# Second sweep of the down projection: pairs in another order, the other accumulators added in two halves, gains on GpSimd, and row tile 0 scaled by two engines

## The reference

```
u = rms_norm(x, ln2) @ w_ffn_in              # 2048 x 11264
a, b = split(u)
g = gelu(causal_depthwise_conv(a)) * b       # 256 x 5632
x = x + g @ w_ffn_out                        # 5632 x 2048: the down projection
y = rms_norm(x, ln_f)                        # x * rsqrt(mean(x^2) + eps) * ln_f
```

## Time and profile before

| what | value |
|---|---|
| median of three executions | 1091.71 us |
| the profiled execution's own time | 1091.31 us |
| its span, first to last instruction | 1089.5 us |
| busy: TensorE, VectorE, ScalarE, GpSimd | 1077.2, 831.9, 602.1, 81.7 us |
| share of TensorE in the span | 99% |
| DMA rate over the span | 253 GB/s |
| mean granted TensorE clock | 0.997 of full speed |

### The profile page before, as it was taken

One profiled execution on the slowest core, in us unless ns is written; L12 is line 12 of the kernel. 1 busy time (PEld: TensorE's weight loads), 2 busy tenths in 40 slices (PEclk: granted clock), 3 DMA queues, 4 the chain that ended last, 5 costly groups with the idle time before them and its releaser, 6 DMA issues.

```text
span 1089.5 us, 16759 instructions
## 1 busy us (share of the span) xinstructions
PE 1077.2 (99%) x5777; PEld 920.9 (85%) x5777; DVE 831.9 (76%) x1117; ACT 602.1 (55%) x810; POOL 81.7 (7%) x86
## 2 busy tenths in 40 slices
PE   9999999999999999999999999999999999999996
PEld 7888888888888888888888888888888888888884
DVE  5755777666768577968879678686798988888897
ACT  7445555555555454544545445455454777777774
POOL 2000111111100000101101011010010100000000
PEclk9999999999999999999999999999999999999998
DMA  9766555555599688797897987978877599969992
GB/s 341 267 190 191 162 168 159 155 171 166 165 317 357 177 267 305 229 337 252 281 320 233 318 266 254 355 209 321 285 236 276 179 315 323 301 223 317 319 325 102
DMA packets 163352, 276.06 MB, mean 253 GB/s; under 512 B 9091, under 2 KB 77537, under 8 KB 159984
## 3 DMA queue, kind: packets, MB, share of 16 engines
q1 hardware_dynamic: 162448, 273.39, 75.5%
q0 software_dynamic: 544, 1.69, 0.4%
q10 hardware_dynamic: 320, 0.47, 0.1%
HBM read 248.18 MB, written 27.26 MB: 253 GB/s over the span
## 4 chain that ended last, share of the span: by engine, by line
PE 93%; DVE 3%; DMA 2%; ACT 1%; issue 0%; SPq 0%; ACTq 0%; DVEq 0%
PE acc L703 16%; PE acc L611 11%; PE acc L613 11%; PE acc L612 11%; PE acc L711 8%; PE bank_s L703 8%; PE bank_tr L703 8%; PE bank_tr L711 4%; PE bank_s L711 4%; DMA raw<-in_w_ffn_out 1%; PE bank_s L613 1%; PE bank_s L611 1%; PE bank_s L612 1%; PE bank_tr L613 1%; PE bank_tr L612 1%; PE bank_tr L611 1%
## 5 line engine op out<-in xcount | busy, mean ns | idle before, releaser
L974 ACT ACTIVATE w_hi<-raw 128x1024 fp32r<-128x1024 f32 x292 | 309.5, 1061 | 404.6 <-PE acc L613 135.7
L1271 DVE TENSOR_TENSOR w_lo<-raw,w_hi 128x1024 fp32r<-128x1024 f32 x292 | 356.1, 1224 | 186.4 <-ACT w_hi L974 185.5
L703 PE MATMUL acc<-h_both,w_hi 128*128 128x512 f32 x768 | 238.4, 392 | 0.0
L703 PEld LDWEIGHTS acc<-h_both,w_hi 128*128 128x128 f32 x768 | 137.9, 189 | 23.2 <-DVE rstd_row L1649 0.2
L711 PE MATMUL acc<-h_both,w_lo 128*128 128x256 f32 x768 | 154.2, 282 | 0.0
L711 PEld LDWEIGHTS acc<-h_both,w_lo 128*128 128x128 f32 x768 | 125.9, 191 | 7.5
L703 PE MATMUL bank_s<-h_both,w_hi 128*128 128x512 f32 x384 | 118.6, 390 | 0.0
L703 PE MATMUL bank_tr<-h_both,w_hi 128*128 128x512 f32 x384 | 118.6, 390 | 0.0
L611 PE MATMUL acc<-w_hi,h_both 128*128 128x512 f32 (+1 forms) x288 | 111.9, 389 | 0.9 <-DVE h_both L1285 0.9
L613 PE MATMUL acc<-w_hi,h_both 128*128 128x512 f32 (+1 forms) x288 | 109.0, 378 | 0.0
L612 PE MATMUL acc<-w_lo,h_both 128*128 128x512 f32 (+1 forms) x288 | 108.8, 378 | 0.0
(11 more groups left out here) (278 smaller groups left out, 1722.9 us busy)
## 6 DMA issues: line engine op xcount, KB each, us to landing
raw<-in_w_ffn_in SPq DMA_DIRECT2D x176, 512.0 KB, 4.4
raw<-in_w_in SPq DMA_DIRECT2D x130, 256.0 KB, 3.0
raw<-in_w_ffn_out SPq DMA_DIRECT2D x64, 512.0 KB, 6.2
stage<-in_w_ffn_out SPq DMA_DIRECT2D x24, 1024.0 KB, 8.2
kept_sums<-stage SPq DMA_DIRECT2D x24, 1024.0 KB, 6.7
raw<-kept_sums SPq DMA_DIRECT2D x24, 768.0 KB, 6.0
raw<-in_w_out SPq DMA_DIRECT2D x32, 512.0 KB, 4.7
raw<-in_w_in SPq DMA_DIRECT2D x19, 512.0 KB, 9.2
```

The lines of the kernel that those rows point to most:

```text
L703: ins = mm(banks[ft // 2][:, ft % 2, :], w_hi[:, slot, q * COLS + ft * P:q * COLS + (ft + 1) * P], h_both[:, 2 * k + q, :, :].rearrange("p ...
L974: run(w_hi[:, n % SPLIT, :], raw[:, n % RAW, :], ACT.Copy).then_inc(hi_ready, 1)
L1271: tt(w_lo[:, n % SPLIT, :], raw[:, n % RAW, :], w_hi[:, n % SPLIT, :].bitcast(F32), ALU.subtract).then_inc(lo_ready, 1)
```

## The change

Five things, all in the second sweep and at its end:

1. The second sweep's pairs come in another order (`ORDER`, `k_pair`). Before, its sevens stood at r = 25, 26, 28, 29, 31, 32, 34, 35, 37, 38, 40, 41. Now they stand at r = 24, 25, 27, 28, 30, 31, 32, 34, 35, 37, 38, 39, and r = 40 to 43 are eights. So twice three sevens follow one another.
2. The other accumulators of the second sweep are added at r = 41 (three additions) and r = 42 (three more), after the low parts of these steps, where they wait for r = 39.
3. The load of `ln_f` is issued behind the loads of r = 40, and ahead of those of r = 41.
4. The four products of the first sweep's blocks with `ln_f` go from VectorE (r = 40) to GpSimd, which makes them as soon as `ln_f` has landed.
5. The last eight products of row tile 0 come in another order, so that m = 86 is needed at the fifth instead of the third product. The second part of row tile 0 is scaled by VectorE, between the 1/rms of row tile 0 and the additions of row tile 1, instead of by ScalarE.

```diff
-X_OUT_AT = (21, 43)
-GAIN_AT = 18
+SECOND_SEVENS = [2, 3, 5, 6, 8, 9, 10, 12, 13, 15, 16, 17]
+SECOND_EIGHTS = [at for at in range(DOWN_PAIRS) if at not in SECOND_SEVENS]
+ORDER = [list(range(DOWN_PAIRS)), [0] * DOWN_PAIRS]
+for at, p in zip(SECOND_SEVENS, S_PAIRS):
+    ORDER[1][at] = p
+for at, p in zip(SECOND_EIGHTS, [p for p in range(DOWN_PAIRS) if p not in S_SLOT]):
+    ORDER[1][at] = p
+FIRST_SEVEN = (S_PAIRS[0], DOWN_PAIRS + SECOND_SEVENS[0])
+LAST_SEVEN = (S_PAIRS[-1], DOWN_PAIRS + SECOND_SEVENS[-1])
+X_OUT_AT = (21, 41)
+LNF_AT = 40
+LNF_BEHIND = 37
+def k_pair(pair):
+    return ORDER[pair // DOWN_PAIRS][pair % DOWN_PAIRS]
...
             for r in range(LAST_PAIR + 1):
                 load_pair(r)
-                if r == DOWN_PAIRS + 14:
-                    sp.wait_ge(g_lo_ready, DOWN_PAIRS + 12)
+                if r == LNF_AT:
+                    sp.wait_ge(g_lo_ready, LNF_BEHIND)
                     sp.dma_start(lnf_row[:], ln_f.partition_broadcast(P)).then_inc(lnf_landed, 16)
-            for t, part, ready, count in ((0, Y_PARTS0[0], y_by_act, 1), (0, Y_PARTS0[1], y_by_act, 2),
-                                          (1, Y_PARTS1[0], y_by_dve, 1), (1, Y_PARTS1[1], y_by_dve, 2)):
+            for t, part, ready, count in ((0, Y_PARTS0[0], y_by_act, 1), (0, Y_PARTS0[1], y_by_dve, 1),
+                                          (1, Y_PARTS1[0], y_by_dve, 2), (1, Y_PARTS1[1], y_by_dve, 3)):
...
-            for c, m in ((0, 84), (0, 85), (0, 86), (1, 84), (1, 85), (1, 86), (0, 87), (1, 87)):
+            for c, m in ((0, 84), (0, 85), (1, 84), (1, 85), (0, 86), (0, 87), (1, 86), (1, 87)):
                 if c == 0:
                     pe.wait_ge(lo_ready, DOWN_TILE + 2 * (m // 2) + 2)
...
                 if (c, t) == (BLOCKS - 1, 0):
                     act.wait_ge(rstd_ready, 3)
-                    act.wait_ge(scaled, TOK * 2 + 2)
+                    act.wait_ge(gained_by_pool, 2 * TOK)
                     scale_out(0, Y_PARTS0[0])
-            scale_out(0, Y_PARTS0[1])
...
-                if r in X_OUT_AT:
-                    others_out(r // DOWN_PAIRS)
+                if r == X_OUT_AT[0]:
+                    others_out(0, 0)
+                    others_out(0, 1)
+                if r in (X_OUT_AT[1], X_OUT_AT[1] + 1):
+                    others_out(1, r - X_OUT_AT[1])
...
-                if r == DOWN_PAIRS + GAIN_AT:
-                    dve.wait_ge(lnf_landed, 16)
-                    for i in range(2 * TOK):
-                        times_gain(i // TOK, i % TOK, i + 1)
...
                 if c == BLOCKS - 1:
                     last_inverse_rms(t, TOK + TOK * BLOCKS + TOK * 2 + i + 1)
+                if (c, t) == (BLOCKS - 1, 0):
+                    dve.wait_ge(rstd_ready, 3)
+                    dve.wait_ge(scaled, 2)
+                    ts(y_tok[:, 0, Y_PARTS0[1]], y_tok[:, 0, Y_PARTS0[1]], rstd[:, 0:1], None, ALU.mult
+                       ).then_inc(y_by_dve, 1)
...
+            def times_gain(c, t, count):
+                own = slice(c * COLS, (c + 1) * COLS)
+                pool.wait_ge(ffn_added, count)
+                nc.gpsimd.tensor_tensor(y_tok[:, t, own], x_res[:, t, own], lnf_row[:, own], ALU.mult
+                                        ).then_inc(gained_by_pool, 1)
             pool.wait_ge(lnf_landed, 16)
-            pool.wait_ge(ffn_added, TOK * BLOCKS)
-            nc.gpsimd.tensor_tensor(y_tok[:, t, own], x_res[:, t, own], lnf_row[:, own], ALU.mult).then_inc(scaled, 1)
+            for i in range(2 * TOK):
+                times_gain(i // TOK, i % TOK, i + 1)
+            times_gain(*LAST_BANKS[-1], TOK * BLOCKS)
```

More of the change, by code:

```diff
@@ L434, in build @@
         scaled = sem("scaled")
+        gained_by_pool = sem("gained_by_pool")
         y_by_act = sem("y_by_act")
@@ L489, in load_pair @@
             def load_pair(r):
-                sweep, p = divmod(r, DOWN_PAIRS)
+                sweep, p = r // DOWN_PAIRS, k_pair(r)
                 use, first = raw_use(r), PAIR_SLOT[r]
@@ L915, in down_pair @@
                 if is_seven(r):
-                    seven_products(r, banks, others, p == S_PAIRS[0], p == S_PAIRS[-1])
+                    seven_products(r, banks, others, r in FIRST_SEVEN, r in LAST_SEVEN)
                 else:
@@ L940, in _ @@
             for r in range(DOWN_PAIRS):
-                if r == S_PAIRS[0]:
+                if r == FIRST_SEVEN[0]:
                     pe.wait_ge(b_sum_ready, GROUPS * 2)
@@ L1165, in g_round @@
                 if is_seven(r):
-                    ins = run(part_hi(r)[:, 4:7, :], g_sums[:, S_SLOT[r % DOWN_PAIRS]], ACT.Copy)
+                    ins = run(part_hi(r)[:, 4:7, :], g_sums[:, S_SLOT[k_pair(r)]], ACT.Copy)
                 ins.then_inc(g_hi_ready, 1)
@@ L1227, in _ @@
                     others = (b_banks, a_banks)[sweep]
-                    act.wait_ge(tile_used, DOWN_TILE + 2 * (sweep * DOWN_PAIRS + S_PAIRS[-1] + 1))
+                    act.wait_ge(tile_used, DOWN_TILE + 2 * (LAST_SEVEN[sweep] + 1))
                     run(u_sum[:], others[0][:, 0, :], ACT.Copy).then_inc(u_ready, 1)
@@ L1670, in lo_pair, with others_out @@
                     tt(sum_lo(r), sum_raw(r), sum_hi(r).bitcast(F32), ALU.subtract).then_inc(t_lo_ready, 1)
-            def others_out(sweep):
+            def others_out(sweep, half):
                 others = (b_banks, a_banks)[sweep]
@@ L1684, in wide @@
                     return ap.unsqueeze(1).broadcast_to([P, 2, COLS])
[L1686 to L1696, removed]
+                if half == 0:
+                    dve.wait_ge(tile_used, DOWN_TILE + 2 * (LAST_SEVEN[sweep] + 1))
+                    dve.wait_ge(u_ready, sweep + 1)
+                    tt(u_sum[:], u_sum[:], x_2, ALU.add).then_inc(x_added, 1)
+                    tt(y11, y11, x_0, ALU.add).then_inc(x_added, 1)
+                    dve.wait_ge(x_added, done + 1)
+                    tt(y_2, y_2, wide(u_sum[:]), ALU.add).then_inc(x_added, 1)
+                else:
+                    tt(y21, y21, u_sum[:], ALU.add).then_inc(x_added, 1)
+                    dve.wait_ge(x_added, done + 3)
+                    tt(y_2, y_2, wide(x_1), ALU.add).then_inc(x_added, 1)
+                    dve.wait_ge(x_added, done + 5)
+                    tt(y2_, y2_, wide(x_3), ALU.add).then_inc(x_added, 1)
             def rest_of_mean(t, before):
@@ L1741, in _ @@
                     last_inverse_rms(t, TOK + TOK * BLOCKS + TOK * 2 + i + 1)
+                if (c, t) == (BLOCKS - 1, 0):
[3 more added lines that the diff above has]
+                       ).then_inc(y_by_dve, 1)
             dve.wait_ge(rstd_ready, 4)
-            dve.wait_ge(scaled, TOK * BLOCKS)
+            dve.wait_ge(gained_by_pool, 2 * TOK)
+            dve.wait_ge(scaled, 3)
             for part in Y_PARTS1[0:2]:
@@ L1804, in _ @@
                 scale_gate(f + 1)
-            c, t = LAST_BANKS[-1]
-            own = slice(c * COLS, (c + 1) * COLS)
+            def times_gain(c, t, count):
[3 more added lines that the diff above has]
+                                        ).then_inc(gained_by_pool, 1)
             pool.wait_ge(lnf_landed, 16)
-            pool.wait_ge(ffn_added, TOK * BLOCKS)
-            nc.gpsimd.tensor_tensor(y_tok[:, t, own], x_res[:, t, own], lnf_row[:, own], ALU.mult).then_inc(scaled, 1)
+            for i in range(2 * TOK):
+                times_gain(i // TOK, i % TOK, i + 1)
+            times_gain(*LAST_BANKS[-1], TOK * BLOCKS)
 def tables():
```

13 lines of the change are left out of this document (7 added, 6 removed).

## The result

The changed kernel takes 1094.37 us (median of 14 runs, 1093.13 to 1095.28), the kernel before 1091.36 us on the same chip (14 runs, 1090.24 to 1092.80). The ratio is 1.0027, with a 95% interval of 1.0019 to 1.0034: slower by some 3 us. The forecast of 1091.3 us with "same" as the likeliest was wrong, and the time lies just inside the upper end of the range. The profiled execution of the changed kernel took 1095.28 us with a span of 1093.5 us, 0.9 us above its median and 4.0 us above the span of before.

The account below looks back on a forecast made before the run. TensorE was taken as the bound, with 93% of the chain. Wait at r = 43 +1.0, end -0.5, stores -0.95 sum to -0.45 us: 1090.9, or 1091.3 us as median; range 1089.0 to 1094.4.

Parts of the forecast that it names:

- Three sevens in a row: Second sweep, twice: loads lose 1.5 us of lead, covered by VectorE's 4.6 us; cost nothing, without that lead 1.5 each.
- the start of the sweep: At r = 24 and 25: 1.9 us of lead left at step 25; cost nothing, else up to 0.5 us.
- Rival D: DMA engines can't feed three sevens in a row; TensorE waits about 1.5 us at two places: 1094.3 us, chance 0.08.
- The load of ln_f: Ahead of r = 41's loads: with the additions at r = 41 and 42, TensorE waits 1.1 us at r = 43.
- Products on GpSimd: Four ln_f products, 5.1 us on GpSimd, hold up VectorE before r = 43 by 0.6 us; bounds 0 and 5.1.
- Rival C: GpSimd's products fall in VectorE's row of 11 us from r = 41 on, up to 1.27 each: 1095.8 us, chance 0.12.
- All four count: By the skill's rule alone, VectorE never idle, all four GpSimd products block it: wait 6.2 us instead of 1.7.
- The wait at r = 43: TensorE waits 1.7 us for VectorE's low part at r = 43's first product, instead of 0.68: +1.0 us.
- The row of 11.04 us: VectorE's unbroken work after r = 41's low part: six additions and the low parts of r = 42 and 43.
- The end and the stores: Last bank's addition no longer lags TensorE's end, -0.5 us; last burst of stores shorter and ending sooner, -0.95 us.

Follow-up runs that it names:

- the best version: Changed kernel with ln_f loaded behind r = 43's loads and its four products on VectorE behind r = 43's low parts: 1089.62 us, ratio 0.9984.
- the repeat: The changed kernel run again with no edit, on the chip on which its variants run: 1094.93 us, ratio 1.0037 to the kernel before.

## Why the prediction was wrong

**Three sevens in a row: the step that failed.** "VectorE's lead on a seven in such a stretch is about 4.6 us ... Cost nothing." The lead was wrong: 4.6 us was r = 35's in the old order, where the sevens begin one step later. With the new start it is 2.0 at r = 28, at most 2.4 from there up to r = 42, and 0.15 at the eights r = 33, 36 and 40, which is a wait; the sevens from r = 25 give 4.8 at r = 28. The prediction's own step on the start of the sweep had the lead down to 1.9 at r = 25 (measured 1.5), and it was not carried on from there. The old order was no safe source either: its leads at r = 37 and 41 are 1.9 and 0.4. The waits at r = 33, 36 and 40, 1.9 us together, come with this low lead; that the wait at r = 40 is not ln_f's is seen in the best version, where r = 40's high part comes as late (1054.33 against 1054.36) without ln_f's load beside it. The loss of up to 1.5 us at each place is near the 1.8 of the run with the sevens from r = 25, but there two sevens in a row take 1.6 as well. Rival D named such waits, close to their places, for another reason: the stretch is fed, only from too small a stock. The time lies inside the range because the range was drawn up to D.

How much of the 3 us the low lead costs by itself is not shown. Two executions with the same low lead at r = 28 had no wait at all (the additions at r = 43; ln_f last and the halves later), the best version keeps it, and of the two runs that restored it neither was faster than its counterpart (ratios 1.0000 against 0.9998, 0.9997 against 0.9986). The changed kernel with only its sevens one step later was not run. What the runs do show is that the loss is gone when ln_f's load moves back (1.0000), when the additions do (0.9998), and turns into a gain when ln_f and the products move together (0.9984).

**The load of ln_f.** r = 38's lead was taken from r = 35's as well (2.9 us; it was 0.6). The delay itself was right: 11.6 us from the sums to r = 41's high part against 11.8 taken. By the step's own sum, r = 41's low part should have ended at T40 + 3.65 and ended at T40 + 4.85; counted from T38 it is 2.2 late, of which TensorE's own wait at r = 40 hid 1.0. The bound "about 3" for ln_f held: 2.2 to 2.4.

**Products on GpSimd.** 0.6 was taken, 1.1 measured in the row (12.02 against 10.93). The price for a collision (1.09, up to 1.27 taken) was right. Too low was GpSimd's own time: four products take 10.4 us beside a busy VectorE, not 5.1, so they reach 2.9 us beyond T41 (1058.82 + 5.44) instead of ending before it. Rival C's mechanism is real, but one product of four was paid in the changed kernel, two to four where ln_f landed later. The rule cited from the Trainium skill (page "SBUF — State Buffer", section "Who interferes with whom") agrees with these rows in that every instruction that grew has two SBUF inputs and those that read PSUM did not grow (0.68 at 1063.59, beside a product). The Trainium skill's words "fully blocks" stand there with VectorE's two-port modes; of an instruction with two SBUF inputs it says that it contends, for ports under an exclusive lock. Not every one with two SBUF inputs grew, though: r = 41's low part took 2.32 us in the midst of the products, and there it was GpSimd that lost time (10.37 us for four). "All four count" came out only where all four met VectorE's row.

**The wait at r = 43.** Forecast 1.7, measured 2.8: 1.2 more from the late low part, 0.4 more from GpSimd, less some 0.4 that TensorE came later itself. The row of 11.04 us was right (10.93 and 10.92). The mechanism was the one forecast, and its size was off through the lead.

**The clock.** It was no term of the sum. After waits of 2.6 to 2.8 us the granted clock fell in two profiled executions (0.57 and 0.62) and not in two others (1.00 in the repeat and in the run without three in a row). It can account for the profiled execution's excess over its median, not for the verdict.

**The end and the stores** were right: -0.5 and -0.95 forecast, -1.66 measured together; the last addition no longer lags, and the burst takes 2.9 us (2.7 forecast).

For the repeat, where the clock stayed full, the sum is +4.6 for the waits, -1.7 for the end and -0.1 for the start: +2.8, the difference of the spans and close to that of the medians.

**Open.** Why TensorE's wait at r = 40 varies from none to 2.6 us between executions of kernels that are alike up to there; in the two runs that kept 2.5 us or more at most steps TensorE did not wait before r = 41. Why the kernel without three in a row is no slower than before. And when the clock falls.

## What to carry to other kernels

A lead is a stock: it belongs to the order and the step in which it was measured, and in a new order it has to be counted again from the start of the dense stretch, step by step. A large load that nobody needs soon should go behind the loads that the next steps wait for, not just ahead of the first one that looks free. Moving work to GpSimd cost VectorE up to 1.1 us for each 512-column product that met it; making the four products itself cost it 2.49 us in all, so VectorE kept ahead by doing them where TensorE did not wait for it.

## What was not expected of the hardware

A GpSimd product of 512 columns took 1.26 us alone and about 2.6 on average (10.37 for four) beside a busy VectorE, so both engines lose. A VectorE instruction with two SBUF inputs that met a product grew by up to 1.1 us, nearly the same whether it takes 0.68 or 2.28 alone, or it did not grow (2.29 at r = 40 and 2.32 at r = 41 in the changed kernel), and then the product took the longer. TensorE's granted clock was near its lower level for some 4 us behind waits of 2.6 and 2.8 us in two executions, and full behind waits of 2.7 and 2.8 us in two others.
